# Gate scatter as two fp32r products of one selector, with a fourth selector operation in each unit

## The reference, cut to what matters

```python
e = i1 * PEER_NKEYS + i2                 # 128 experts picked per token out of 128 * 128
gate = jax.nn.softmax(cv, axis=-1)
act = jax.nn.gelu(jnp.einsum('td,thkd->thk', xb, u_tab[e]), approximate=False)
return jnp.einsum('thk,thkd->td', gate * act, v_tab[e])
```

## Time and profile before

| what | value |
|---|---|
| time, median of three runs | 4009.47 us |
| the profiled execution: span, first to last instruction | 3988.8 us |
| median less that span (start and end of an execution) | 20.7 us |
| granted TensorE clock, mean over the span | 0.983 |
| busy share PE, PEld, DVE, ACT, POOL | 97, 87, 72, 39, 57% |
| scatter on PE (L1419), both layers | 161.3 us in 1280 instructions |
| the three selector operations on DVE (L2706, L2707, L2709), both layers | 99.5, 99.6 and 101.8 us in 80 each |

### The profile page before, as it was taken

The page is one execution under the profiler, slowest core; times in us unless marked ns, Lnnn a source line. Parts: engine busy times, 40 slices in busy tenths (PEclk is TensorE's granted clock), DMA queues, the critical chain, the costliest instruction groups (busy, mean ns, idle before and its releaser), DMA issues.

```text
span 3988.8 us, 59456 instructions
## 1 busy us (share of the span) xinstructions
PE 3877.4 (97%) x23204; PEld 3461.4 (87%) x23204; DVE 2869.6 (72%) x4841; ACT 1540.6 (39%) x2349; POOL 2259.3 (57%) x1452
## 2 busy tenths in 40 slices
PE   8999999999999999999999999999999999999999
PEld 6778599999999999999477876999999999999994
DVE  5764368955887878888567552799458887798885
ACT  1443145553333334444314432555532333343343
POOL 0032069887777657668101310888877774688861
PEclk9988999999999999999999899999999999999999
DMA  4201146666899999999221021566679899999992
GB/s 122 52 13 48 43 170 215 214 233 218 305 322 320 316 361 388 395 395 343 78 66 39 12 75 43 188 214 210 220 246 312 304 322 333 346 383 380 378 340 71
DMA packets 417975, 900.99 MB, mean 226 GB/s; under 512 B 94496, under 2 KB 242208, under 8 KB 416032
## 3 DMA queue, kind: packets, MB, share of 16 engines
q1 hardware_dynamic: 272288, 552.91, 40.2%
q0 software_dynamic: 90112, 268.76, 18.7%
q10 hardware_dynamic: 55296, 75.52, 5.2%
HBM read 773.87 MB, written 123.15 MB: 225 GB/s over the span
## 4 chain that ended last, share of the span: by engine, by line
PE 52%; POOL 15%; DMA 14%; DVE 11%; issue 5%; ACT 2%; SPq 0%; DVEq 0%; ACTq 0%; POOLq 0%
PE banks L1364 11%; PE banks L826 7%; PE banks L1376 7%; POOL peer_gates L2079 6%; PE banks L1438 5%; DMA u_stage<-peer_ut 5%; POOL u_stage L2095 4%; PE banks L1473 4%; DMA gated<-dense_gelus 3%; PE banks L1275 3%; POOL u_stage L2087 3%; DMA peer_gates<-peer_v,u_stage 3%; PE banks L1293 3%; DVE normed L2729 2%; DMA normed<-peer_ut 1%
## 5 line engine op out<-in xcount | busy, mean ns | idle before, releaser
L2079 POOL DMA_INDIRECT peer_gates<-peer_v,u_stage x512 | 733.8, 1433 | 387.3 <-DVE normed L2729 157.6
L1438 PE MATMUL banks<-gated_parts,v_parts 128*128 128x320 f32 x6144 | 911.1, 310 | 19.9 <-DVE gated_parts L2776 18.2
L1438 PEld LDWEIGHTS banks<-gated_parts,v_parts 128*128 128x128 f32 x6144 | 905.8, 189 | 25.4 <-issue 25.2
L1364 PE MATMUL banks<-peer_x_parts,u_parts 128*128 128x448 f32 x3168 | 664.0, 367 | 3.3 <-DVE u_parts L2715 3.3
L1364 PEld LDWEIGHTS banks<-peer_x_parts,u_parts 128*128 128x128 f32 x3168 | 590.5, 188 | 49.6 <-DVE u_parts L2715 4.1
L2095 POOL DMA_INDIRECT u_stage<-dense_gelus,u_stage x256 | 374.5, 1463 | 106.9 <-issue 77.4
L1364 PE MATMUL banks<-peer_x_parts,low_s 128*128 128x448 f32 x1696 | 398.3, 367 | 0.5 <-DVE low_s L2715 0.5
L2729 DVE SCALAR_TENSOR_TENSOR normed<-peer_gates,u_stage,normed 128x1024 f32<-128x1024 f32 x254 | 327.5, 1289 | 85.3 <-DMA peer_gates<-peer_v,u_stage 71.0
L2745 DVE SCALAR_TENSOR_TENSOR peer_gates<-peer_gates,u_stage 128x1024 f32<-128x1024 f32 x254 | 325.4, 1281 | 81.3 <-DMA peer_gates<-peer_v,u_stage 71.3
L1869 ACT ACTIVATE u_stage<-banks 128x448 f32<-128x448 f32 x256 | 139.2, 544 | 621.8 <-PE banks L1364 616.8
L2087 POOL DMA_INDIRECT u_stage<-gelus,u_stage x256 | 329.0, 1285 | 78.1 <-issue 78.0
(11 more groups left out here) (355 smaller groups left out, 6642.6 us busy)
## 6 DMA issues: line engine op xcount, KB each, us to landing
v_stage<-peer_v SPq DMA_DIRECT2D x256, 512.0 KB, 7.7
u_stage<-peer_ut SPq DMA_DIRECT2D x244, 512.0 KB, 5.2
dense_gelus<-u_stage ACTq DMA_DIRECT2D x256, 224.0 KB, 5.3
gates<-peer_gates SPq DMA_DIRECT2D x16, 2560.0 KB, 20.3
u_stage<-gates SPq DMA_DIRECT2D x64, 640.0 KB, 8.9
gated<-dense_gelus SPq DMA_DIRECT2D x256, 160.0 KB, 7.6
x<-peer_ut SPq DMA_DIRECT2D x64, 512.0 KB, 4.7
u_raw<-peer_ut SPq DMA_DIRECT2D x64, 512.0 KB, 4.9
```

What stands on the lines that cost most here:

```text
L1364: ins = mm(PS[:, d % 2, 0:DW], u_part(n, a, k), XR[:, b, k, DENSE0:TOK], start=(k == 0 and m == 0), stop=(k == KT - 1 and m == 2))
L1438: ins = mm(vc[k][:, 0:PW3], VR[:, s, b, k * 128:(k + 1) * 128], HR[:, s, a, :], start=(j == 0 and m == 0), stop=(j == NKEYS - 1 and m == 2))
L2079: eng.indirect_dma_start(out=GU[:, t % 4, :], out_offset=None, in_=din["peer_v"].rearrange("l i j d -> (l i j) d"), in_offset=bass.Indirec ...
```

## The change

The gate plane is split once a layer into a high part `GHI`, rounded to fp32r, and the rest, which stays in `IT`. A unit then makes the 0/1 selector of the first number once, and from it two weighted selectors, `OHH` (high gates) and `OHL` (low gates, in place). PE does two fp32r products into the same 128 columns of PSUM, both with `OH2` as weights, where it did one fp32 product. `oh_chosen` now counts twice a unit, and the last multiply waits for the one before it. The two selectors of the first number stay where both were; the two of the second number move into the region of the scores, one of them where `PICKSUM` begins, for which the first `add_picked` gets a wait.

```diff
--- before.py
+++ after.py
@@ -266,9 +266,6 @@
     SQX = region(4, TOK)
     assert place["at"] <= KT * TOK - 2 * 4 * 128
     place["at"] = 0
-    OH1 = region(2, 8, 128)
-    OH2 = region(2, 8, 128)
-    place["at"] = 0
     UA = region(4, D)
 
     phase = ExitStack()
@@ -369,6 +366,7 @@
     UC = region(2, D)
     place["at"] = 0
     GBUF = region(2, NKEYS, GBLK)
+    oh2_at = place["at"]
     place["at"] = UNION - 5 * D
     PICKSUM = region(D)
     GU = region(4, D)
@@ -427,9 +425,18 @@
     HIGH_N = region(2, D)
     memory(phase, "parts_a", KT * TOK, F32R)
     PARTS_A = region(4, D)
+    place["at"] = 0
+    OHL = region(2, 8, 128)
+    OHH = region(2, 8, 128)
     memory(phase, "high_c", UNION, F32R)
     place["at"] = HEADS * TOK
     HIGH_C = region(2, D)
+    place["at"] = oh2_at
+    OH2 = [region(8, 128)]
+    GHI = region(PW3)
+    assert place["at"] <= UNION - 5 * D
+    place["at"] = UNION - 5 * D
+    OH2.append(region(8, 128))
     memory(phase, "x_parts_gap", 2 * KT * TOK)
     memory(phase, "u_raw", 4 * D)
     RAW_U = region(2, 2, D)
@@ -1416,8 +1423,9 @@
                     if u >= 2:
                         pe.wait_ge(gates_copied, 2 * n + q - 3)
                     for t in range(4):
-                        ins = mm(PS[:, 4 + (u % 2) * 2 + q, t * 128:(t + 1) * 128], OH2[:, u % 2, 4 * q + t, :],
-                                 OH1[:, u % 2, 4 * q + t, :], start=True, stop=True)
+                        out, row = PS[:, 4 + (u % 2) * 2 + q, t * 128:(t + 1) * 128], OH2[u % 2][:, 4 * q + t, :]
+                        mm(out, row, OHH[:, u % 2, 4 * q + t, :], start=True, stop=False)
+                        ins = mm(out, row, OHL[:, u % 2, 4 * q + t, :], start=False, stop=True)
                     ins.then_inc(scattered, 1)
                 for q in rows_of_unit(u):
                     dense_row(NF + q)
@@ -2689,6 +2697,10 @@
                     dve.did(TT(g3, g3, bc(GSUM[:, 8:8 + H_], 2, TOPK), ALU.mult).then_inc(dve_done, 1), "igt", L, i)
             for i in SPREAD:
                 dve.wait_ge(act_done, at("drained", "it", L, i))
+            dve.did(TS(GHI, IT[:, 2], 1.0, None, ALU.mult).then_inc(dve_done, 1))
+            dve.wait_ge(dve_done, count("dve_done"))
+            dve.did(TT(IT[:, 2], IT[:, 2], GHI.bitcast(F32), ALU.subtract).then_inc(dve_done, 1))
+            dve.wait_ge(dve_done, count("dve_done"))
 
             def gathered(t):
 
@@ -2703,10 +2715,13 @@
                 if u >= 2:
                     dve.wait_ge(scattered, 2 * n - 2)
                 it = lambda c: bc(IT[:, c, 8 * u:8 * u + 8], 2, 128)
-                TT(OH1[:, u % 2], bc(const("iota"), 1, 8), it(0), ALU.is_equal).then_inc(oh_chosen, 1)
-                TT(OH2[:, u % 2], bc(const("iota"), 1, 8), it(1), ALU.is_equal)
-                dve.wait_ge(oh_chosen, n + 1)
-                TT(OH1[:, u % 2], OH1[:, u % 2], it(2), ALU.mult).then_inc(oh_ready, 1)
+                chosen, high = OHL[:, u % 2].bitcast(F32), bc(GHI.bitcast(F32)[:, 8 * u:8 * u + 8], 2, 128)
+                TT(OHL[:, u % 2], bc(const("iota"), 1, 8), it(0), ALU.is_equal).then_inc(oh_chosen, 1)
+                TT(OH2[u % 2], bc(const("iota"), 1, 8), it(1), ALU.is_equal)
+                dve.wait_ge(oh_chosen, 2 * n + 1)
+                TT(OHH[:, u % 2], chosen, high, ALU.mult).then_inc(oh_chosen, 1)
+                dve.wait_ge(oh_chosen, 2 * n + 2)
+                TT(OHL[:, u % 2], chosen, it(2), ALU.mult).then_inc(oh_ready, 1)
 
             def low_u(q):
 
@@ -2740,6 +2755,7 @@
                 gathered(t)
                 w = WGT[:, m:m + 1]
                 if m == 0:
+                    dve.wait_ge(scattered, 2 * UNITS * (L + 1))
                     ins = TS(PICKSUM, GU[:, t % 4, :], w, None, ALU.mult)
                 else:
                     ins = STT(PICKSUM, GU[:, t % 4, :], w, PICKSUM, ALU.mult, ALU.add)
```

## The result

| | before | after |
|---|---|---|
| median of 6 runs, us | 4009.12 (4002.53 to 4013.12) | 4045.35 (4035.08 to 4055.4) |
| ratio of times | | 1.0092, 95% interval 1.006 to 1.0124 |
| profiled execution: span, us | 3988.8 | 4053.6 |
| first to fortieth scatter, layers 0 / 1, us | 461.7 / 462.5 | 480.3 / 476.7 |

The change costs 36 us (24 to 50). The forecast was 4039, and the mechanism came: DVE holds PE up. Where in the stage it does so came out otherwise than forecast.

What follows compares the result with a forecast made beforehand. DVE was to become the bound, 48.5 us in four units against PE's 46.1. +35 us, less the start and PE's 2 us hidden, gave +29: span 4017.8, plus 20.7, said as 4039; range 3998 to 4080.

Steps and rivals of the forecast that it cites:

- PE gains nothing: PE's scatter at L1419: 16 fp32r products at 108 ns, 1.73 us a unit in place of 1.70.
- DVE +1.28 us a unit: Fourth selector operation on DVE: 1.135 us of pace plus 0.14 for the new wait, 102 us over 80 units.
- The wait for the fourth row stays at 3.3 us: DVE's four-row steps: POOL gets no looser, so the 3.3 us wait for the fourth gathered row stays.
- The start gives back 3 us a layer: Stage start: DVE begins a unit ahead and first steps lack gathered rows, giving back some 3 us a layer.
- POOL's rule: POOL's gathers: 0.94 us beside DVE's gathered rows, 1.97 beside its two-input operations; pace 1.25 against 2.26.
- The sum for the stages: Both stages: +1.8 us in four units, 9.75 fours a layer, +35 us; less the start's give-back, +29 us.
- PE's waits by DVE, 8 to 20 us a layer: Before L1419, PE's idle time by DVE would rise from some 8 us to some 20 a layer.
- GHI, the moved selectors and the added wait hidden: Layer start and selectors: `GHI` hidden by DVE's 51.2 us idling; moved selectors and `PICKSUM`'s wait cost nothing.
- The 20.7 us between span and median: Whole kernel: 20.7 us between profiled span and median of runs, added to span 4017.8 to give 4038.5.
- Slack takes it all: Rival, chance 0.18: DVE's idle time in the stage absorbs the added operation, giving 4009 to 4015 us.
- Faster by PE's stream: Rival, chance 0.13: L1419's products at 62 ns, scatter 1.0 us a unit in place of 1.70, giving 3985 us.
- Dear products: Rival, chance 0.12: a narrow fp32r product costs 213 ns like fp32, PE's unit 13.2 us, giving 4116 us.

Runs made afterwards that it cites:

- The products alone: The changed kernel without the operation that makes the high selector, both fp32r products reading `OHL`: 4010.46 us, ratio 1.0002 to the kernel before.
- The multiply by itself: The kernel before, fp32 scatter kept, with a fourth multiply a unit on DVE that nobody reads, and the change's chain of waits: 4039.03 us, 1.0066.
- the gap alone: The kernel before with the unread fourth multiply on DVE only in the first six units of each layer: 4014.79 us, 1.0005.
- the second execution of before: The kernel before, unedited, run and profiled again: 4014.6 us, 1.0003; stage 464.4 / 465.5 us.
- 18 lead gathers: `LEAD` 18 in place of 24 weight gathers before the first row: in the changed kernel 4026.06 us, 1.0023; in the kernel before 4000.57 us, 0.9962.
- one product: The changed kernel without the high selector and with only the product of `OHL`, 8 scatter instructions a unit: 3994.7 us, 0.9972 to the kernel before.

## Why the prediction was right, step by step

- **PE gains nothing: right.** 1.73 us a unit was said, 1.74 measured. The products alone leave the time at 1.0002 (0.9972 to 1.0032). That it does not shrink with the columns fits a pace set by the weight load: the Trainium skill, "TensorE: Matmul & The Clock Gate", section LDWEIGHTS, gives 107 ns for 128 columns, and the trace's 109 agrees; the 81 ns of its section Back-to-back issue gap did not come.
- **DVE +1.28 us a unit: right**, 1.27 in the selector part and in the three-row step 10.96 against 10.98. The multiply by itself costs 26 of the 36 us. The other 10 are within the two intervals, and I did not part them.
- **The wait for the fourth row stays at 3.3 us: failed.** I kept it because POOL gets no looser. But DVE comes later to each row, and the row has mostly landed: 1.32 in the step shown, 35.2 down to 17.8 us in the first layer's stage. The rule under it was too neat as well: beside DVE's gathered rows a gather does not always take 0.94 us (see the last section). Four units on DVE are 3 x 10.96 + 13.64 = 46.5, not 48.5, so DVE and PE (46.1) are near level. "DVE becomes the bound" overstates it: it leads in some steps. That half of the rival in which slack takes it was at work.
- **The start gives back 3 us a layer: failed, with the wrong sign.** It costs 12.8 and 9.5 us, of which 3.9 and 3.4 are PE's lower clock in the sixth period, a term that the sum did not have. I had POOL's rule (0.94 or 1.97 us a gather) and used it for four steady units, but not for the 24 gathers ahead of the first row, where 4 us more on POOL meet a DVE and a PE that have no other work. What the gap costs in time is less than it measures: with the gap alone the time was the old one (1.0005, 0.9984 to 1.0025).
- **The sum for the stages: 29 us predicted, 32.7 measured, by two errors that cancel.** Steady units were said at +35 and gave +10; the start was said at -6 and gave +22. So the nearness of 4039 to 4045 is in part luck. How much the steady units give is not sharp: against the second execution of before, and with 18 lead gathers, they give +20. Periods came at 12.3 and 12.2 as said, but as a mean over most at 11.5 and two at 15 to 21. A mean period does not tell the two apart; the list of periods does.
- **PE's waits by DVE, 8 to 20 us a layer: right in size** (18.3 and 17.8), with half of the first in one wait. ACT's rounded rows shrank as said: 33.7 to 25.0 and 57.3 to 33.4.
- **GHI, the moved selectors and the added wait hidden: right** as far as a run shows it. The products alone keep all three and stay at 1.0002.
- **The 20.7 us between span and median**, taken as fixed, is mostly the quickness of that one execution. The profiled run of after, 4055.4, is 1.8 us above its span of 4053.6, and the table's "start and end of an execution" is therefore some 2 us and not 20.7. Using it as an offset did no harm, since it only set the level to the median.
- **Rivals.** Slack takes it all: fell. Faster by PE's stream: fell at its price (62 ns, 109 measured), and one product shows that even with half the products gone the gain is some 11 us and not clear of noise. Dear products: fell.

Open: why PE issues slowly around the third or fourth unit in some kernels and executions, which costs 8 to 30 us a stage; where the 15 us of 18 lead gathers come from; and what binds the kernel with one product. In its stage of layer 0 the chain of waits names POOL's two gathers for 25%, the row gathers' landing for 11%, the loads of `u_tab` rows for 17% and PE's dense rows for 9%.

## What to carry to other kernels

When work moves to an engine with 20% idle time, price it by what the waits behind it do: the same operation was worth 13, 26 and 44 us as the slack went. Then look at the start of the stage apart from its steady part, by listing the periods: queues that are filled ahead (here 24 gathers) may be just in time before the change and late after. Such a count is a knob to try by itself; here 18 for 24 gained 15 us (5 to 26) with no other edit. And list the periods of two executions of the same kernel first: what differs between them is no effect of a change.

## What was not expected of the hardware

- An operation of two per-partition scalars with 128 columns has a pace of 0.26 us on DVE (8 in 2.07 us, starts 1183.92 and 1185.99), where the same columns inside one wide operation cost 0.14 (1.135 / 8). And beside it POOL's gather took 0.94 us, not the 1.97 of the earlier trace rows:

```profile
1183.92 2.31 DVE L2709 TENSOR_SCALAR x<-kept,u_stage 128x128 f32<-128x128 f32 x8
1185.99 1.21 DVE L2716 TENSOR_TENSOR u_parts<-u_stage,u_parts 128x1024 fp32r<-128x1024 f32 x1
```

```profile
1183.99 0.94 POOL L2087 DMA_INDIRECT u_stage<-gelus,u_stage  x1 [0.30 <-issue]
```

- The Trainium skill, "SBUF — State Buffer", section "Who interferes with whom", says that a DVE instruction with two SBUF inputs contends with a GpSimd instruction that reads SBUF. The trace agrees in part. Before, all 71 gathers that lie beside the three selector operations alone take 1.95 to 1.97 us. But the gathered rows have two SBUF inputs as well, and beside them both lengths occur: in the stage of layer 0, 59 of 74 such gathers take under 1.2 us before, and 26 of 49 over 1.8 us after. One of these and the rows beside it, after:

```profile
1208.75 1.94 POOL L2087 DMA_INDIRECT peer_gates<-peer_v,u_stage  x1 [0.58 <-DVE normed L2744]
```

```profile
1207.15 4.11 DVE L2744 SCALAR_TENSOR_TENSOR normed<-peer_gates,u_stage,normed 128x1024 f32<-128x1024 f32 x3
```

What decides between the two lengths no run here shows.

- PE can issue slowly with nothing to wait for. In the kernel before, run again, in its fourth period:

```profile
958.03 0.27 PE L1419 MATMUL banks<-x 128*128 128x128 f32 x1 [0.93 <-issue]
```
